# A decoder step on one core: index products in units 3 and 4, a float32r token projection, top-k rounds dealt out anew, and the bias table skewed sooner

## The reference

```python
def a_project(x, w_in, idx_g, idx_b):
    q, k, v, qi, ki, wi = jnp.split(x @ w_in, A_SPLIT_POINTS, axis=-1)
    ...
    ki = layer_norm(ki, idx_g, idx_b)

def dsa_attend(q, qi, wi, q_pos, idx_keys, gather_kv, topk, table):
    s = jnp.einsum('bqhe,bse->bqhs', qi.astype(jnp.float32), idx_keys.astype(jnp.float32))
    score = jnp.einsum('bqhs,bqh->bqs', jax.nn.relu(s), wi.astype(jnp.float32)) * IDX_SCALE
    admissible = jnp.arange(L, dtype=jnp.int32)[None, :] <= q_pos[:, None]
    score = jnp.where(admissible[None], score, NEG)
    _, idx = lax.top_k(score, topk)
    ...
    logits = jnp.where(valid[:, :, None, None, :], logits + bias, NEG)
    p = jax.nn.softmax(logits, axis=-1).astype(v_sel.dtype)
```

## Time and profile before

| | |
|---|---|
| median of 3 runs | 1247.8 us (1246.69 to 1247.99) |
| profiled execution, its own time | 1249.62 us |
| its span, first to last instruction | 1247.6 us |
| PE busy | 1199.7 us, 96% |
| DVE busy | 708.1 us, 57% |
| mean granted PE clock | 0.992 of full |
| layer 0's projections (units 0 to 13) | 33.2 to 146.9 us of the span |
| output projection starts | 259.75 us |

### The profile page before, as it was taken

How to read it: one execution, slowest core, us unless ns; L and a number is a source line. 1 busy time by engine, 2 the same in 40 slices (tenths; PEclk the granted TensorE clock), 3 DMA queues, 4 the chain that set the end, 5 groups by cost and what they waited for, 6 DMA issues and landing times.

```text
span 1247.6 us, 25437 instructions
## 1 busy us (share of the span) xinstructions
PE 1199.7 (96%) x9582; PEld 1106.5 (89%) x9582; DVE 708.1 (57%) x1456; ACT 477.1 (38%) x873; POOL 82.5 (7%) x117
## 2 busy tenths in 40 slices
PE   8998988899999999999999999999999999999995
PEld 4958854589999999999999987798999999999994
DVE  2289899857843442443457767678533433433477
ACT  2342166634531331322334566644422322412332
POOL 4434300100030000000000000000000000000000
PEclk9999999999999999999999999899999999999998
DMA  6698580233122222222223211131222222222222
GB/s 208 189 286 264 163 234 2 72 117 102 51 85 100 86 87 99 84 100 85 88 100 107 80 55 51 52 136 35 85 85 92 93 85 101 84 88 97 85 85 69
DMA packets 61960, 129.97 MB, mean 104 GB/s; under 512 B 7819, under 2 KB 34603, under 8 KB 61755
## 3 DMA queue, kind: packets, MB, share of 16 engines
q1 hardware_dynamic: 47899, 115.16, 27.5%
q10 hardware_dynamic: 10624, 7.21, 2.0%
q0 software_dynamic: 3360, 6.56, 1.7%
HBM read 124.36 MB, written 9.79 MB: 108 GB/s over the span
## 4 chain that ended last, share of the span: by engine, by line
PE 81%; DVE 14%; ACT 2%; issue 2%; DMA 0%; SPq 0%; DVEq 0%; ACTq 0%
PE PS L616 61%; PE PS L648 7%; PE PS L1034 3%; PE PS L846 2%; PE PS L793 2%; PE PS L806 2%; DVE YA L1658 2%; PE PS L820 2%; DVE YA L1645 1%; DVE PB L1796 1%; DVE RSTD L1650 1%; DVE SC L1955 1%; DVE MX L1953 1%; DVE X L1664 1%; DVE PB L1821 1%
## 5 line engine op out<-in xcount | busy, mean ns | idle before, releaser
L1501 DVE TENSOR_TENSOR WLO<-WRAW,WHI 128x1024 fp32r<-128x1024 f32 x118 | 145.3, 1231 | 322.2 <-ACT WHI L1096 322.2
L1096 ACT ACTIVATE WHI<-WRAW 128x1024 fp32r<-128x1024 f32 x126 | 133.4, 1059 | 387.4 <-PE PS L616 351.6
L616 PE MATMUL PS<-XH,WHI 128*128 128x260 f32 x1184 | 241.5, 285 | 0.9 <-DVE XL L1828 0.7
L616 PE MATMUL PS<-XH,WLO 128*128 128x260 f32 x1184 | 239.1, 284 | 0.0
L616 PE MATMUL PS<-XL,WHI 128*128 128x260 f32 x1184 | 238.6, 283 | 0.0
L616 PE MATMUL PS<-HH,WHI 128*128 128x260 f32 x944 | 191.2, 284 | 0.2 <-DVE HL L1525 0.2
L616 PE MATMUL PS<-HH,WLO 128*128 128x260 f32 x944 | 190.2, 283 | 0.0
L616 PE MATMUL PS<-HL,WHI 128*128 128x260 f32 x944 | 189.9, 283 | 0.0
L616 PEld LDWEIGHTS PS<-XH,WHI 128*128 128x128 f32 x1184 | 183.1, 189 | 6.4 <-issue 5.4
L616 PEld LDWEIGHTS PS<-XH,WLO 128*128 128x128 f32 x1184 | 183.0, 189 | 0.0
L616 PEld LDWEIGHTS PS<-XL,WHI 128*128 128x128 f32 x1184 | 182.7, 189 | 0.0
(11 more groups left out here) (293 smaller groups left out, 1868.8 us busy)
## 6 DMA issues: line engine op xcount, KB each, us to landing
WRAW<-wall SPq DMA_DIRECT2D x168, 512.0 KB, 3.2
bias_skewed<-bias_seq SPq DMA_DIRECT2D x4, 1280.0 KB, 17.6
BT<-bias_skewed ACTq DMA_DIRECT2D x3, 1024.0 KB, 8.8
X<-xT SPq DMA_DIRECT2D x4, 520.0 KB, 7.0
X<-xT SPq DMA_DIRECT2D x1, 2080.0 KB, 11.1
yT<-X SPq DMA_DIRECT2D x8, 260.0 KB
KVB<-cacheK SPq DMA_DIRECT2D x16, 128.0 KB, 3.2
KVX<-cacheK SPq DMA_DIRECT2D x16, 128.0 KB, 3.2
```

The lines of the kernel that those rows point to most:

```text
L616: mm = pe.matmul(PS[:, 2 * slot + g, 0:TG], w[:, slot, k, :], x[:, k, TG * g:TG * g + TG], start=(k == 0 and w is WHI and x is hi), stop=( ...
L1096: nc.scalar.activation(WHI[:, slot], WRAW[:, slot], ACT.Copy).then_inc(hi_done, 1)
L1501: V.tensor_tensor(WLO[:, slot], WRAW[:, slot], WHI[:, slot].bitcast(F32), ALU.subtract).then_inc(lo_dve, 1)
```

## The change

1. The token projection is done in float32r like the units: ACT also makes `WNH` of the weights and DVE `WNL`, and PE multiplies in four quarters of two k each (hi·hi, then lo·hi and hi·lo), 120 products for 40.
2. The index products run in units 3 and 4, three before each even k, ordered by head pair, so that they need only the units evicted so far. `sample_scores` and `sample_sums` go to k=2 and k=4 of unit 5.
3. SP loads units 2 and 3 between its index pages, leaves the weights out of `early(1, s)`, and issues the skew DMAs behind `early(2, s)`, ahead of the loads of units 6, 7 and 8.
4. `SLOT_OF` begins one slot sooner (ahead of k=4 of unit 6). `low_part(6)` stands ahead of the first rounds. The rounds are dealt out anew: 9 first (10 before), one with each digit and each step, then 4, 6, 1, 5 (5, 5, 1, 7 before), and in steps 0 to 11 of the attention two halves each (before: none in 0 and 1, one in 2 to 5, two in 6 to 11).
5. ACT reads the page numbers of one sample per unit in units 6 to 12 where it read all at unit 6.

```diff
-SLOT_OF = (2, 3, 4, 5, 6, 7, 8, 9, 12, 13, 14)
+SLOT_OF = (1, 2, 3, 5, 6, 8, 9, 10, 12, 13, 14)
...
-            with sp.Fori(4 - IDX_SP, 4) as c:
+            for c in range(4 - IDX_SP, 4):
                 for pg in range(NPG):
                     load_index_page(sp, 1, c, pg, idx_sp)
+                u = c + IDX_SP - 2
+                sp.wait_ge(lo_dve, u - 1)
+                load_unit(u, u % 2)
...
-            with sp.Fori(1, POOL_LO[0] // 2) as i:
-                for s in range(2):
-                    early(i, s)
-            early(POOL_LO[0] // 2, 0)
+            for s in range(2):
+                early(1, s, weights=False)
+            for s in range(2):
+                early(2, s)
             sp.wait_ge(toe_out, 16)
             for i0 in range(0, P, 32):
                 sp.dma_start(bass.AP(tensor=bskew.tensor, offset=i0 * (NH * SKEW + 1),
...
+            for s in range(2):
+                early(3, s)
+            early(POOL_LO[0] // 2, 0)
             early(POOL_LO[0] // 2, 1)
...
+            for q in range(4):
+                pe.wait_ge(nat_hi, q + 1)
                 for t in range(5):
...
+                    for k in (2 * q, 2 * q + 1):
+                        natural(t, k, XH, WNH, start=(k == 0))
+                pe.wait_ge(nat_lo, q + 1)
+                for t in range(5):
+                    for k in (2 * q, 2 * q + 1):
+                        natural(t, k, XL, WNH)
+                        mm = natural(t, k, XH, WNL, stop=(k == KT - 1))
...
-            items = [(t, h) for t in range(1, QT) for h in range(IDXH)]
+            items = [(t, h + e) for h in range(0, IDXH, 2) for t in range(1, QT) for e in range(2)]
...
-                if u == 5:
-                    between = {k: (lambda k=k: index_scores(3 * k, 3 * k + 3))
-                               for k in range(KT)}
-                elif u == 6:
-                    between = {2: sample_sums}
+                if u in (3, 4):
+                    n = 12 * (u - 3)
+                    between = {k: (lambda n=n + 3 * k // 2: index_scores(n, n + 3))
+                               for k in range(0, KT, 2)}
+                elif u == 5:
+                    between = {2: sample_scores, 4: sample_sums}
...
-            ins.then_inc(x_hi, 1)
+                if q == 3:
+                    ins.then_inc(x_hi, 1)
+                nc.scalar.activation(WNH[:, k, :], WN[:, k, :], ACT.Copy).then_inc(nat_hi, 1)
...
+                V.tensor_tensor(WNL[:, k, :], WN[:, k, :], WNH[:, k, :].bitcast(F32),
+                                ALU.subtract).then_inc(nat_lo, 1)
...
             for n, (t, h) in enumerate(items):
-                if n == 8:
-                    low_part(6, 0)
-                if n == 16:
-                    sample_queries()
+                if n == 4:
+                    low_part(4, 0)
+                if n == 13:
+                    low_part(5, 1)
...
-            prompt_rounds(10)
-            low_part(7, 1)
+            low_part(6, 0)
+            prompt_rounds(9)
             dve.wait_ge(ds_ev, 1)
...
-                prompt_rounds(1)
+                prompt_halves(2)
+                if r == 0:
+                    low_part(7, 1)
...
-                prompt_rounds(1 if i else 2)
+                prompt_rounds(1)
...
-            prompt_rounds(5)
+            prompt_rounds(4)
...
-            prompt_rounds(5)
+            prompt_rounds(6)
...
                 if i == -1:
-                    prompt_rounds(7)
-                elif i >= 2:
-                    prompt_halves(2 if 6 <= i < 12 else 1)
+                    prompt_rounds(5)
+                else:
+                    prompt_halves(2)
```

More of the change, by code:

```diff
@@ L230, in program @@
         KVI = place("KVI", [P, 2, NPG, 256], at=hw)
+        WNH = place("WNH", [P, KT, NATW], F32R, at=0)
+        WNL = place("WNL", [P, KT, NATW], F32R, at=KT * NATW)
         BT0 = place("BT0", [P, NH, P], at=0)
@@ L344, in program @@
         nat_mm, nat_ev = sem("nat_mm"), sem("nat_ev")
+        nat_hi, nat_lo = sem("nat_hi"), sem("nat_lo")
         kstat, ksd, kid = sem("kstat"), sem("ksd"), sem("kid")
@@ L484, in _, with early @@
             sp.wait_ge(x_lo, 1)
-            def early(i, s):
-                sp.wait_ge(lo_dve, i * 2 + (s - 1))
-                load_unit(i * 2 + s, s)
+            def early(i, s, weights=True):
+                if weights:
+                    sp.wait_ge(lo_dve, i * 2 + (s - 1))
+                    load_unit(i * 2 + s, s)
                 for n in ((4, 5), (0, 1))[s]:
@@ L838, in prompt_attention, with natural @@
                         output(i - 1)
-            for k in range(KT):
-                if k % 2 == 0:
-                    pe.wait_ge(x_in[k // 2], 32)
-                for t in range(5):
[L845 to L848, removed]
+            def natural(t, k, x, w, start=False, stop=False):
+                m = P if t < QT else DB
+                return pe.matmul(PS[0:m, t, 0:NATW], x[:, k, t * P:t * P + m], w[:, k, :],
+                                 start=start, stop=stop)
+            for q in range(4):
+                pe.wait_ge(nat_hi, q + 1)
+                for t in range(5):
+                    for k in (2 * q, 2 * q + 1):
[6 more added lines that the diff above has]
+                    if q == 3:
                         mm.then_inc(nat_mm, 1)
@@ L862, in index_scores @@
                     t, h = items[n]
+                    if t == 1 and h % 2 == 0:
+                        pe.wait_ge(ev_act, h // 2 + 1)
                     if n >= 4:
@@ L1330, in _ @@
             nc.scalar.activation(KSD[:], KMV[:, :, 1], ACT.Sqrt, bias=EPSC[:]).then_inc(ksd, 1)
-            items = [(t, h) for t in range(1, QT) for h in range(IDXH)]
+            items = [(t, h + e) for h in range(0, IDXH, 2) for t in range(1, QT) for e in range(2)]
+            numbers = {}
             for u in range(STATIC_UNITS):
-                if u == 5:
-                    for n, (t, h) in enumerate(items):
+                if u in (3, 4):
+                    for n in range(12 * (u - 3), 12 * (u - 3) + 12):
+                        t, h = items[n]
                         act.wait_ge(is_mm, n + 1)
@@ L1340, in _ @@
                                              ).then_inc(is_relu, 1)
-                if u == 6:
-                    numbers = page_numbers(act, 2, V_HALF + V_LATE)
+                if 6 <= u < 13:
+                    numbers.update(page_numbers(act, 2, (V_HALF + V_LATE)[u - 6:u - 5]))
+                if u == 5:
                     for n, (c0, c1) in enumerate(((0, 512), (512, 1024), (1024, 1025))):
@@ L1363, in _ @@
                                          ).then_inc(ev_act, 1)
-                if u == 2:
+                if u == 1:
                     act.wait_ge(kit_mm, 1)
@@ L1909, in sample_queries @@
                 ins.then_inc(qib_ready, 1)
-            items = [(t, h) for t in range(1, QT) for h in range(IDXH)]
-            for u in range(2, 6):
+            items = [(t, h + e) for h in range(0, IDXH, 2) for t in range(1, QT) for e in range(2)]
+            for u in range(2, 4):
                 low_part(u, u % 2)
@@ L1926, in _ @@
                 wi = NAT[:, t, HD + h:HD + h + 1]
+                if n:
+                    dve.wait_ge(is_acc, n)
                 if h == 0:
@@ L1933, in _ @@
                 ins.then_inc(is_acc, 1)
-                dve.wait_ge(is_acc, n + 1)
+            sample_queries()
+            dve.wait_ge(is_acc, len(items))
             for t in range(1, QT):
```

14 lines of the change are left out of this document (8 added, 6 removed).

## The result

The changed kernel took 1255.08 us (median of 4 runs, 1254.51 to 1257.07) beside 1247.89 us (4 runs, 1246.69 to 1248.62): 7.2 us slower by the medians; the ratio of the two kernels' runs on record is 1.0068 with a 95% interval of 1.0049 to 1.0087. That ratio is not the quotient of the two medians (1.0058), and 0.0068 of the kernel before is 8.5 us, so a microsecond or so either way is not known. The forecast was 1252.4 us, slower by 4.6. The profiled execution, 1255.42 us, has a span of 1253.6 us, 6.0 more than before.

The account below looks back on a forecast made before the run. The bound was taken to change hands before the output projection, DVE setting the pace in the attention. Terms: -1.2 us to unit 13's end, +5.8 for the rounds, +4.6 in all: 1252.4 us, range 1242.0 to 1257.0.

Parts of the forecast that it names:

- Token projection: PE's first stage in float32r: end near 28 us, 4 us sooner, kept only if no later load is late.
- rival (d): The float32r projection is no shorter, its quarters waiting for ACT and DVE; 0.22 shared with rival (a) and a middle way.
- W: When unit 6's weights land behind the skew copies: 82.4 to 85.6 us, taken as 84.
- rival (b): In balance: W between 77 and 82 us, time within 0.2% (2.5 us); chance 0.18.
- Digit 0: DVE's first indicator, 12.9 us after W: at 96.9 us, only 1.5 us sooner than before.
- The wait of some 10 us: PE's expected standstill ahead of digit 0, with 1.4 us more for a low clock behind it.
- From digit 0 to the end of unit 13: Before 48.5 us; now 46.2, plus 1.2 for unit 7's low part and 1.4 for low clock: end at 145.7 us.
- the two waits: PE's waits for an indicator in the projections before, 1.42 and 1.94 us, expected not to return: 3.4 us saved.
- rival (c): POOL's low parts again stall DVE's small updates (+3.4 us), W 85.6 (+1.6): 1257.4 us; inside the forecast's 0.60.
- The rounds: Eight halves added in attention steps 0 to 5 cost 6.1 us of DVE time: +5.8 us net.
- Rival (a): Copies do not delay unit 6: weights by 73.4 us, indicator at 86.4, 1240.6 us; 0.22 with rival (d) and a middle way.
- This is the step that I think decides: Skew copies issued from about 54.5 us instead of 75.84, so loads of units 6, 7 and 8 queue behind them.

Follow-up runs that it names:

- e4: Kernel before with only the float32r token projection added: 1252.30 us, ratio 1.0039.
- e12: Kernel before with the float32r projection and units 2 and 3 loaded between SP's index pages; skew copies, index products and rounds unchanged: 1241.58 us, ratio 0.9957.
- e1: Changed kernel with the four skew copies put back behind the pages of unit 8: 1255.82 us, ratio 1.0078.
- e9: Changed kernel with the skew copies on SP in two pairs, behind the pages of units 7 and 8: 1249.05 us, ratio 1.0029.
- e7: Changed kernel with the skew copies issued on ACT's queue, behind units 1, 2 and 3, instead of SP's: 1259.72 us, ratio 1.0117.
- e11: Changed kernel with POOL's low parts of units 8 to 13 cut to one of eight k, output wrong: 1248.90 us, ratio 1.0021.
- e5: Changed kernel with the attention's old halves and 13 rounds instead of 9 ahead of the digits: 1252.54 us, ratio 1.0058.
- e6: Changed kernel with the attention's old halves, and nine rounds ahead of unit 6's low part, four behind it: 1244.67 us, ratio 1.0000.
- e8: Changed kernel with skew copies on ACT's queue, the attention's old halves, 12 rounds ahead of the digits and 6 at step -1: 1254.98 us, ratio 1.0079.
- e10: Changed kernel with skew copies in two pairs, the attention's old halves, 12 rounds ahead of the digits and 6 at step -1: 1245.03 us, ratio 0.9999.
- e2: Changed kernel with the first nine rounds ahead of unit 6's low part instead of behind it: 1249.89 us, ratio 1.0032.
- e3: Kernel before with only the four skew copies moved ahead of the loads of units 6, 7 and 8: 1269.48 us, ratio 1.0209.

## Why the prediction was right, point by point

1. **Token projection**, 4 us: measured 4.1, and 0.147 to 0.151 us a product, so rival (d) is out. That it lasts only while no load is late is shown by e4 (lost) and e12 (kept).
2. **W**, 84 us from 26.6 to 29.8 us for the copies: 81.9. That the load stood in line behind the copies is shown by its landing 1.9 us behind the last of them while POOL's pages took 6.1 us, by e1 and e9, where without the four copies ahead of it it was in time, and by unit 4's load in e7, which overtook a copy on another queue. The lower of the two estimates was the better one. By the forecast's own figures a W of 81.9 us belongs to rival (b), no change within 2.5 us.
3. **Digit 0**, 96.9 us: 94.45. The 12.9 us from W to there were 12.6. The wait of some 10 us that PE was to have ahead of it was 0.86 and 2.48 us; the low clock behind it came even so.
4. **From digit 0 to the end of unit 13**: this is the step that was mis-sized. "Neither the two waits (-3.4) nor the low clock (-1.4) need come back: 46.2 us", with 1.2 and 1.4 on top, gave 48.8; measured were 53.5. Waits of 1.57, 1.70 and two of 0.2 us came back, 3.7 us in all, and behind the last long one a second stretch of low clock, 1.4 us. The 1.2 us for `low_part(7)` did not show as a wait, since PE itself came late out of the first low stretch. e11 shows the cause: with POOL's low parts made small, these waits are gone, and 5.2 us with them. It was rival (c), which I had priced at 3.4 us and left out of the sum. Points 2 and 3 were 2.4 us on the good side and hid half of it. That the time came out near the forecast, though W was in rival (b)'s range, is in part luck: an early W and a term put at nothing offset each other.
5. **The rounds**, +5.8 us, of which 6.1 for the steps and -0.3 for an earlier start: the steps took 5.8 us more, the first transposes came 0.7 us sooner behind unit 13, +5.1 together. With the old halves 78.9 us in e5, e6, e8 and e10 against 84.1 to 84.5 us with the new ones, the steps' part is shown.
6. **Sum**: +4.6 forecast. By the traces +1.0 to the end of unit 13 and +5.1 from there, +6.0 by the spans; +7.2 by the medians.
7. **Rival (a)** was wrongly priced. With unit 6 in time it put the indicator at 86.4 us and took that for the sum on PE. In e1 the indicator was at 87.1, but PE, with the index and sample products ahead of it, came to the slot at 90.2 (and in e9 at 91.0). So the late W cost PE 4.3 us at this slot, not the 10.5 that lie between the forecast's two figures. Nor is W the only load that counts: in e1 unit 9's cost the gain. "This is the step that I think decides" is therefore too much said of the skew copies: with them put back behind unit 8, the time stays as it is (e1), and what decides the sign is shared between them, the collisions and the rounds (e9, e11 and e6 against e2 take back 4.9, 5.9 and 4.0 us by the ratios, which overlap and do not add up). The sum did not rest on (a).

What stays open: the medians differ by 1.2 us more than the profiled spans. The runs of one kernel lie 1.4 to 15 us apart, and I have profiles of one execution each, so how often a DVE operation meets a POOL one, and how often the clock goes down, is not known. The move of the index products and that of ACT's page numbers were not run by themselves.

## What to carry to other kernels

A queue that feeds an engine just in time must not be given a long transfer in one piece: ask for each load behind it when it is wanted, and split the long one so that each stays within that time (e9), since moving the block only changes which load is late (e1, e3, e7). A gain early in a chain is worth what the next late arrival leaves of it; move the loads with it (e12 against e4). Work taken from a place where its engine waits and put where the same engine sets the pace costs nearly its full time (5.8 us for halves of 6.1).

## What the runs showed of the hardware that I had not expected

PE's granted clock goes down to 0.50 (1.2 of 2.4 GHz) after short waits, not only after long ones: after 1.94 us in the kernel before, 1.70 us in the changed one, 2.19 us in e4, 1.58 us in e9 (at 120.55). The low stretch behind them lasted some 3.5 us, but 10 us in e4, with PE busy throughout. It does not follow every such wait: in the kernel before there was none after the 2.34 us at 171.48, and in the changed one none after the 1.57 us at 125.69. The wait of 2.14 us ahead of the second transposes of the attention is the same in six runs; the low clock follows it in the changed kernel, e2, e7 and e9, and not in e1 and e11. So the length of the wait alone does not tell.

The collision of DVE with POOL is not bound to two inputs. The operation of 2.45 us at 121.13 us is a TENSOR_SCALAR with one input from memory. The Trainium skill, "SBUF — State Buffer", section "SBUF: two separate sides", puts such stalls down to a pair of ports that one engine holds for a whole instruction, for operations with two inputs and for some modes of DVE. All four long stalls in the two traces (2.16 to 2.45 us) and the two shorter ones of the changed kernel end with POOL's operation, within 0.2 us, and agree with that. Whether this TENSOR_SCALAR ran in such a mode, no trace here shows.
